# Finer waits in four stages of a two-block transformer kernel, and added products of constants on TensorE

## What is computed

```
h = rmsnorm(x, norm1_g);  proj = h @ w_in                 # 1024 x 3100, 16 parts
o_a = hgrn2(...)                                          # gated linear recurrence, 4 heads
o_b = nsa(...)                                            # compressed + selected + window attention, 8 heads
o_c = fox(...)                                            # attention with decay, 4 heads
x = x + concat(o_a, o_b, o_c) @ w_o
x = x + square(relu(rmsnorm(x, norm2_g) @ w_up)) @ w_down # 1024 -> 4096 -> 1024
```

## Time and profile before

| | |
|---|---|
| time, median of 3 | 3463.31 us |
| profiled execution, its own time | 3466.33 us |
| its span in the profile | 3465.1 us |
| TensorE busy (PE, matmul) | 3244.2 us, 94% |
| VectorE busy (DVE) | 2226.9 us, 64% |
| ScalarE busy (ACT) | 1802.8 us, 52% |
| GpSimd busy (POOL) | 374.9 us, 11% |
| moved by DMA | 590.90 MB, mean 171 GB/s |
| mean granted clock of TensorE | 0.974 |

### The profile page before, as it was taken

One profiled execution on the slowest core, in us unless ns is written; L12 is line 12 of the kernel. 1 busy time (PEld: TensorE's weight loads), 2 busy tenths in 40 slices (PEclk: granted clock), 3 DMA queues, 4 the chain that ended last, 5 costly groups with the idle time before them and its releaser, 6 DMA issues.

```text
span 3465.1 us, 42078 instructions
## 1 busy us (share of the span) xinstructions
PE 3244.2 (94%) x16598; PEld 2685.4 (77%) x16599; DVE 2226.9 (64%) x3404; ACT 1802.8 (52%) x2699; POOL 374.9 (11%) x333
## 2 busy tenths in 40 slices
PE   8899999999989999999989999999789899999995
PEld 6789778877789787878677777788677878888784
DVE  5756442436856443434666888899743669998886
ACT  3334342323334342324463788788633638887884
POOL 1111000000111000000140111111100101111110
PEclk9989999999989999999999999999889999999998
DMA  4210222221120222222104899898722258999995
GB/s 141 74 58 1 73 97 94 86 88 50 62 70 1 74 97 73 98 90 88 55 1 165 350 354 353 345 367 351 291 73 109 77 198 332 366 361 355 359 358 184
DMA packets 135161, 590.90 MB, mean 171 GB/s; under 512 B 29744, under 2 KB 35632, under 8 KB 110256
## 3 DMA queue, kind: packets, MB, share of 16 engines
q1 hardware_dynamic: 115664, 569.85, 42.6%
q0 software_dynamic: 19296, 18.30, 2.2%
HBM read 594.34 MB, written 44.04 MB: 184 GB/s over the span
## 4 chain that ended last, share of the span: by engine, by line
PE 36%; DMA 6%; DVE 5%; ACT 3%; issue 1%; SPq 0%; POOL 0%; DVEq 0%; ACTq 0%; POOLq 0%
PE ps L190 32%; DMA mem<-in_w_up 5%; PE ps L3430 1%; DMA mem<-in_w_gate 1%; ACT r L3495 1%; DVE r L3550 1%; PE ps L3471 1%; DVE mem L2637 0%; PE ps L2521 0%; ACT mem L3520 0%; ACT mem L2580 0%; DVE r L2951 0%; PE ps L3162 0%; DMA xa<-mem,memu 0%; DVE mem L3789 0%
## 5 line engine op out<-in xcount | busy, mean ns | idle before, releaser
L190 PE MATMUL ps<-r,r 128*128 128x512 f32 (+2 forms) x10920 | 2576.5, 395 | 70.9 <-DVE r L2151 23.2
L190 PEld LDWEIGHTS ps<-r,r 128*128 128x128 f32 (+1 forms) x10920 | 2026.9, 190 | 540.3 <-issue 53.5
L3550 DVE TENSOR_TENSOR r<-mem,r 128x1024 fp32r<-128x1024 f32 x768 | 902.6, 1221 | 132.5 <-ACT r L3495 126.0
L3495 ACT ACTIVATE r<-mem 128x1024 fp32r<-128x1024 f32 x768 | 788.1, 1061 | 222.4 <-PE ps L190 141.7
L703 ACT ACTIVATE r<-mem 128x512 fp32r<-128x512 f32 (+3 forms) x518 | 340.8, 666 | 901.7 <-PE ps L190 892.7
L738 DVE TENSOR_TENSOR r<-mem,r 128x512 fp32r<-128x512 f32 (+1 forms) x256 | 174.9, 688 | 428.4 <-ACT r L703 427.0
L740 DVE SCALAR_TENSOR_TENSOR r<-mem,r 128x512 fp32r<-128x512 f32 (+3 forms) x262 | 183.7, 717 | 279.6 <-ACT r L703 277.8
L3408 POOL DMA_INDIRECT xa<-mem,memu x64 | 102.5, 1601 | 964.4 <-ACT mem L3520 949.8
L3348 POOL DMA_INDIRECT mem<-xd,memu x64 | 96.3, 1505 | 57.8 <-PE ps L3430 34.4
L1929 DVE TENSOR_REDUCE mem<-ps 128x1 f32<-128x512 f32 (+3 forms) x160 | 67.5, 484 | 43.8 <-PE ps L1674 40.9
L1716 PE MATMUL ps<-mem 128*128 128x65 f32 x800 | 95.4, 275 | 0.0
(11 more groups left out here) (408 smaller groups left out, 2794.7 us busy)
## 6 DMA issues: line engine op xcount, KB each, us to landing
mem<-in_w_up SPq DMA_DIRECT2D x80, 2048.0 KB, 18.6
mem<-in_w_down SPq DMA_DIRECT2D x80, 2048.0 KB, 8.0
mem<-in_w_gate SPq DMA_DIRECT2D x64, 2048.0 KB, 13.4
mem<-in_w_in SPq DMA_DIRECT2D x10, 2048.0 KB, 7.9
mem<-in_odd_w_qkv SPq DMA_DIRECT2D x6, 2048.0 KB, 10.8
mem<-in_w_o SPq DMA_DIRECT2D x4, 2048.0 KB, 13.1
mem<-in_rel SPq DMA_DIRECT2D x16, 512.0 KB, 3.3
mem<-in_even_w_in SPq DMA_DIRECT2D x3, 2048.0 KB, 8.6
```

The source lines that it names most:

```text
L190: r = e.matmul(out, a, b, start=start and i == 0, stop=stop and i == n - 1, skip_group_check=skip)
L3495: act.e.activation(wh, w, ACT.Copy).then_inc(*self.S["ex_wh"](self.l, e, i))
L3550: dve.e.tensor_tensor(wl, w, wh.bitcast(F32), SUB).then_inc(*self.S["ex_wl"](self.l, e, i))
```

## The change

- `Ffn.ready`: the wait for `ff_lo` asks for the block that the product uses.
- Projection: the first compression matrix is loaded in two halves into columns 3072 to 4095 of the buffers of the last two slices; `("cmp", l)` holds the second matrix alone.
- `Causal.dve`: compression steps 52 and 53 of VectorE stand in step 1, before `dve_finish(0)`.
- `Turn.pe`: a product of the identity with itself before each unit, into the bank that the unit then overwrites.
- Experts: the hidden turn of expert 31 stands amid the down products of expert 30, with hidden buffers of its own (a free half of `XH`, `XL`) and results in banks 2 and 3; ScalarE and VectorE take the work for it in another order.
- `Tail.pe`: 6, 2, 2 and 2 products of the identity with 512 columns of constants before units 0, 2, 4 and 6.

```diff
@@ class Kern, layout
+        self.constant = self.hm[:, 0:4, :]
@@ weight chunks
+def with_part(make, src, k):
+    def both(buf):
+        part = buf[:, 3072:4096].rearrange("p (k n) -> p k n", k=8)
+        return make(buf) + [(part, src[1024 * k:1024 * k + 1024, :].rearrange("(k p) n -> p k n", p=128))]
+    return both
...
+            if i >= 4:
+                out["in", l, c] = with_part(out["in", l, c], A["nsa_cmp_w1"][l, 0], i - 4)
...
-        out["cmp", l] = lambda buf, l=l: [
-            (buf[:, 2048 * i:2048 * i + 2048].rearrange("p (k n) -> p k n", k=16),
-             A["nsa_cmp_w1"][l, i].rearrange("(k p) n -> p k n", p=128)) for i in range(2)]
+        out["cmp", l] = lambda buf, l=l: [(buf[:, 0:2048].rearrange("p (k n) -> p k n", k=16),
+                                           A["nsa_cmp_w1"][l, 1].rearrange("(k p) n -> p k n", p=128))]
@@ class Turn, pe
         for u in self.order:
+            pe.e.matmul(self.ps(u)[:, 0, :], self.K.ident, self.K.ident, start=True, stop=True)
             self.pe_unit(pe, u)
@@ class Mixer, compress_pe
-            w1 = K.wbuf(("cmp", l))[:, 2048 * w:2048 * w + 2048].rearrange("p (k n) -> p k n", k=16)
-            K.wait_weights(pe, ("cmp", l))
+            chunk = ("cmp", l) if w else ("in", l, PROJ[4 + half][0])
+            at = 1024 * half if w else 3072
+            w1 = K.wbuf(chunk)[:, at:at + 1024].rearrange("p (k n) -> p k n", k=8)
+            K.wait_weights(pe, chunk)
...
-            mm(pe.e, self.hidden(), [(w1[:, k, :], self.TG[:, :, 2 * k:2 * k + 16 * 30 + 1:16])
-                                     for k in range(8 * half, 8 * half + 8)],
+            mm(pe.e, self.hidden(), [(w1[:, k, :], self.TG[:, :, 2 * k + 16 * half:2 * k + 16 * half + 16 * 30 + 1:16])
+                                     for k in range(8)],
@@ class Causal, dve
+            if n == 1:
+                self.M.compress_dve(dve, 52)
+                self.M.compress_dve(dve, 53)
             if n:
                 self.dve_finish(dve, n - 1)
-            if n == 2:
-                self.M.compress_dve(dve, 52)
-                self.M.compress_dve(dve, 53)
@@ class Ffn
-                    jobs[-1].half = half
+                    jobs[-1].half, jobs[-1].kq = half, kq
...
-            pe.wait_ge("ff_lo", self.name, 16 * job.half + 15)
+            pe.wait_ge("ff_lo", self.name, 16 * job.half + 8 * job.kq + kk)
@@ class Experts
-        self.HH, self.HL = K.r(o1 + 6144, 512), K.r(o1 + 6656, 512)
+        hidden = [K.r(o1 + 6144 + 512 * i, 512) for i in range(2)]
+        last = [x[NE % 2].rearrange("p k n -> p (k n)")[:, 0:512] for x in (self.XH, self.XL)]
+        self.hidden = [last if e == NE - 1 else hidden for e in range(NE)]
@@ pe_down
-        if e:
+        if e and e < NE - 1:
             pe.wait_ge("ex_y", l, e - 1, 1)
         pe.wait_ge("ex_hl", l, e)
         for i in range(8, 12):
+            if i == 10 and e == NE - 2:
+                self.pe_turn_hidden(pe, NE - 1)
...
+    def result(self, e, n):
+        return self.K.bank[(2 if e == NE - 1 else 6) + n][:, :]
@@ pe
-            if e < NE:
+            if e < NE - 1:
                 self.pe_turn_hidden(pe, e)
@@ act
-            if c == NE and i == 8:
-                self.act_hidden(act, NE - 1)
+            if c == NE and i == 11:
                 self.act_result(act, NE - 2)
             if n >= self.RING:
                 self.act_high(act, n)
+            if c == NE and i == 9:
+                self.act_hidden(act, NE - 1)
@@ dve
-            if c == NE and i == 8:
-                self.dve_hidden(dve, NE - 1)
             if n >= self.RING:
                 self.dve_low(dve, n)
+            if c == NE and i == 9:
+                self.dve_hidden(dve, NE - 1)
@@ class Tail, pe
             for u in range(8):
+                for _ in range((6, 0, 2, 0, 2, 0, 2, 0)[u]):
+                    pe.e.matmul(self.turn.ps(u), self.K.ident, self.K.constant, start=True, stop=True)
                 self.turn.pe_unit(pe, u)
```

More of the change, by code:

```diff
@@ L3458, in pe_down @@
             k = i - 8
-            hh, hl = (a[:, 128 * k:128 * k + 128] for a in (self.HH, self.HL))
+            hh, hl = (a[:, 128 * k:128 * k + 128] for a in self.hidden[e])
             for n in range(2):
                 m = slice(512 * n, 512 * n + 512)
-                r = mm(pe.e, K.bank[6 + n][:, :], ((hh, wh[:, m]), (hl, wh[:, m]), (hh, wl[:, m])), k == 0, k == 3)
+                r = mm(pe.e, self.result(e, n), ((hh, wh[:, m]), (hl, wh[:, m]), (hh, wl[:, m])), k == 0, k == 3)
             r.then_inc(*S["ex_mm"](l, e, i))
+    def result(self, e, n):
+        return self.K.bank[(2 if e == NE - 1 else 6) + n][:, :]
     def pe_turn_hidden(self, pe, e):
@@ L3504, in act_hidden @@
         act.wait_ge("ex_ht", self.l, e)
-        if e:
+        if e and e < NE - 1:
             act.wait_ge("ex_mm", self.l, e - 1, 11)
-        act.e.activation(self.HH, self.K.bank[4][:, :], ACT.Copy).then_inc(*self.S["ex_hh"](self.l, e))
+        act.e.activation(self.hidden[e][0], self.K.bank[4][:, :], ACT.Copy).then_inc(*self.S["ex_hh"](self.l, e))
     def act_silu(self, act, e):
@@ L3519, in act_result @@
         for n in range(2):
-            act.e.activation(self.YY[e % 2][:, 512 * n:512 * n + 512], self.K.bank[6 + n][:, :], ACT.Copy,
+            act.e.activation(self.YY[e % 2][:, 512 * n:512 * n + 512], self.result(e, n), ACT.Copy,
                              scale=self.R.GT[:, e:e + 1]).then_inc(*self.S["ex_y"](self.l, e, n))
@@ L3560, in dve_hidden @@
         dve.wait_ge("ex_hh", self.l, e)
-        dve.e.tensor_tensor(self.HL, self.K.bank[4][:, :], self.HH.bitcast(F32),
+        dve.e.tensor_tensor(self.hidden[e][1], self.K.bank[4][:, :], self.hidden[e][0].bitcast(F32),
                             SUB).then_inc(*self.S["ex_hl"](self.l, e))
```

## The result

The changed kernel takes 3408.21 us (median of 4 runs, 3406.08 to 3410.24), the kernel before beside it 3464.43 us (4 runs, 3461.7 to 3471.0). The ratio is 0.9835, 95% interval 0.9818 to 0.9852: faster by 56 us. The forecast was 3386 us, a gain of 78, and the median lies 3.2 us above the upper end of the range. The direction was right, the size was not.

A forecast was written before the change was run, and what follows sets the result against it. TensorE, busy 94% of the span, bounds the kernel, with some 221 us idle. 32.3 + 19.3 + 12.7 + 11.5 + 0 + 1.8 = 77.6 us off 3466.33 gives 3388.7, forecast 3386 us for timed runs; range 3373 to 3405.

The forecast's parts named there:

- the feed-forward: Finer wait for the hidden values' low part: 23.2 us of idle and 9.1 of half clock go, 32.3 us.
- the causal part: VectorE's compression steps moved earlier: waits of 3.60 us (7.2 in all) and half of 11.1 us go, 12.7 us.
- rival A: Whole kernel: idle time goes but half clock falls on other thin stretches; gain 50, 3413 us; chance 0.10.
- The tail: Behind the experts, products of 512 columns fill TensorE's idle time: clock gained 1.8 us, between −3 and +3.
- the turns: Four turn stages with identity products: cost 3.4 us, half clock behind two worth 3.4; taken as 0, −5 to +3.4.
- The expert ends: Last expert's hidden turn moved amid the products before: last scatter 6.5 us earlier, 5.0 at the kernel's end, together 11.5.
- The projection: Split loading of compression weights: waits of 14.9 us and half of 8.8 us at half clock go, 19.3 us.
- rival D: Feed-forward: the finer wait is followed at once by a wait for a weight piece; gain 45, 3418 us; chance 0.04.
- rival C: Projection: compression halves land late and stop ScalarE, VectorE and TensorE together, so the kernel is slower; chance 0.03.
- ScalarE's result ahead of piece 11: Last expert: ScalarE puts expert 30's result first; piece 11's low part is there at 2488.8, wanted at 2489.3.
- the 45 that the prediction had asked for: Whole kernel: the prediction is wrong if TensorE's idle time falls by less than 45 us.
- Rival B: Turns and tail: added products don't pay, new small waits take 5 us; gain 65, 3398 us; chance 0.22.

The follow-up runs named there:

- e_causal_only: The kernel before with only VectorE's two compression steps of the causal part moved; 3461.3 us, ratio 0.9974.
- e_again: The changed kernel run once more with no edit; 3402.66 us, ratio 0.9813.
- e_turn_fill: The changed kernel without the turns' identity products, with three 512-column products of constants behind the last unit of the three later turns; 3395.97 us, ratio 0.9796.
- e_cmp_only: The kernel before with only the split loading of the compression weights; 3450.99 us, ratio 0.9956.
- e_experts_only: The kernel before with only the last expert's new order; 3458.77 us, ratio 0.9973.
- e_ffn_only: The kernel before with only the feed-forward's finer wait; 3441.19 us, ratio 0.9923.

## Why the prediction was wrong in size

The step that failed is the sum's account of the clock. The prediction says: "So each wait costs its idle time and half of that stretch." It gave each removed wait this price and each stretch elsewhere none. The price itself is right in the feed-forward and the causal part, which are within 0.5 us of it. Missing is the other side, which the prediction had as rival A, "half clock is met elsewhere", with its chance of 0.10 and its mechanism all or nothing. What happened lies between the two: the removed stretches went and paid nearly in full, and new ones came up, at stalls that were there before. They cost 7.7 us net in the profiled execution, 6.4 of them in the causal part. The tail's 1.4 us for a forecast of 1.8 is luck as far as the runs show: e_causal_only has them without the tail's products, and three kernels with these products lost them again. What decides where the new stretches fall stays open.

The second is the turns. "Three stages at 0.75 and the first, at its slow start, at 1.2 cost 3.4 us" and "half clock behind two of these stages is worth 3.4. I take **0**, between −5 and +3.4." Measured +6.3, outside the bounds. The cost at full clock was put too high (third turn 0.55 us, layer 1 in e_again 0.5, where 0.75 was taken). The start cost 1.76 rather than 1.2, of which 1.4 came back before 28 us, where TensorE waited 1.13 us for a load before and no longer does (the −1.4 in the ledger's row on loads). And in the two mix turns the clock fell inside the stage (+2.0 each), which no bound held, while the stretch behind them kept its half clock. The rule of the Trainium skill that was weighed there (page "TensorE: Matmul & The Clock Gate", section "Part 4: PE-mode transpose"), that transposes don't engage the full clock, is not borne out: in the kernel before the pace doubled at the start among transposes alone, 32 transposes ran in 3.68 us in e_turn_fill too, and the identity products amid them didn't keep the clock up in after (7.0 us in both layers). The kernels whose mix turns all ran free of half clock, in the turn and behind, are the two with the idle time filled and e_cmp_only, which has no added product; identity products ahead of the units left 2.01 us of idle time.

Third, mis-sized terms. The expert ends gave 8.4 for 11.5. The prediction let the last scatter start when the one before lands ("Scatter 30 starts by the same rule at 2485.1 + 2.06 = 2487.2 and lands 5 to 5.6 us later (the median of the last two is 5.0)"). The start of scatter 30 was right to 0.3 us. It landed after 6.7 us, and 0.8 us more passed before the next one started; at the kernel's end 6.0 for 6.2, and 0.8 again. The scatter stood 3 us behind the issue of a load and now stands 2 us behind it, and the figure was read from the arrangement that the change undoes. The projection gave 18.0 for 19.3: behind the wait stand 16 products of 93 columns, which took 3.73 us at half clock and 2.73 in after, so full clock gave back 1.0 us there where half of the time would be 1.9. The second expert stage, which the loads of weights pace, varies between executions (against before: −2.3 us in e_experts_only, +0.8 in e_again, +4.2 in after, +4.5 in the kernel before run again); such a spread of single stages belongs into the range and wasn't there.

Right were the mechanisms of the four parts: no wait replaced by another (rival D), compression halves in time (rival C), VectorE's steps early enough, ScalarE's result ahead of piece 11. TensorE's idle time fell by 65 us, more than the 45 that the prediction had asked for. Rival B's time, 3398, is not what happened either: its three charges were turns 3.4, tail 2 and new waits 5; the turns cost more, the tail lost nothing, and no new waits came.

## What to carry to other kernels

Count the idle time of a removed wait in full, but the clock behind it with a discount: small stalls that ran at full clock before can lose it afterwards, so the range for such a change needs a term for new half clock (here 7.7 us elsewhere and 3 in turns, against 18.9 that the feed-forward, projection, causal part and tail gave back beyond their idle time). Where products that nothing reads are to be tried, the idle time behind a chain is a better place than the chain itself: the two kernels with such a fill have the lowest times, though that the fill is the cause isn't shown. Before a clock effect seen in one profile is put down to an edit, look at the same place in profiles of kernels that don't differ there. Where one transfer must land before the next starts, take the landing time from an arrangement like the new one, with what travels beside them, and add the time from landing to start.

## What the hardware showed that was not expected

- The granted clock behind one and the same stall of 1.28 us was 1.00 in three profiles and 0.50, for 3.4 or 6.8 us in one layer or both, in eleven; in e_ffn_only, layer 0, all products up to there are those of before.
- A half clock can begin inside a turn of transposes: 32 of them took 3.68 us or 5.26.
- An indirect scatter landed 6.7 to 6.9 us behind its start with a load of 2 MB issued 2 us ahead (5.6 before, with the load 3 us ahead), 6.0 at the kernel's end (6.3 before), and the next scatter, which waited for it, started 0.8 us later.
- With three products of 512 columns (six instructions, 2.74 us) in the idle time behind a mix turn, four turns of four had no half clock in them or behind; without any product at the turns it was 4 of 16, each over 3.32 us of idle time.
- The entry of the feed-forward had 6.8 us at half clock in layer 1 alone in one profile of the kernel before, and in layer 0 alone in the other.
